# Hybrid attention slots: the product of the probabilities moves ahead of the slot's first delta step

## What is computed

```python
o_a = banded_attention(q_a, k_a, v_a, A_WINDOW, attn_sinks)       # 4 heads, window 128, sink logits
o_b = nsa_mixer(q_b, ...)                                         # 4 heads: compressed, selected, window branch
o_c = gated_delta_net(cqkv, ca, cb, cz, ...)                      # 4 heads of 128, chunks of 64
x = x + gt_m * (concatenate([o_a, o_b, o_c], axis=-1) @ w_out)

# both attentions, for each head and block of 128 queries:
p = softmax(where(mask, q @ k.T * scale, NEG_INF));  o = p @ v

# gated delta rule, for each chunk c of 64 tokens, in sequence:
v_new = u[c] - w[c] @ state
o_c   = q_dec[c] @ state + qk[c] @ v_new
state = state * g_last[c] + k_dec[c].T @ v_new
# before that, u and w come from a triangular solve for each chunk
```

## Time and profile before

| | |
|---|---|
| median of 3 runs | 2823.74 us (2822.07 to 2827.61) |
| the profiled execution's own time | 2822.6 us, its span 2821.1 us |
| PE busy | 2694.4 us (96% of the span) |
| DVE busy | 1626.9 us (58%) |
| ACT busy | 1123.0 us (40%) |
| slots of the first hybrid layer | 1503.2 to 1654.7 us |
| slots of the second hybrid layer | 2243.9 to 2395.4 us |

### The profile page before, as it was taken

The page is one execution under the profiler, slowest core; times in us unless marked ns, Lnnn a source line. Parts: engine busy times, 40 slices in busy tenths (PEclk is TensorE's granted clock), DMA queues, the critical chain, the costliest instruction groups (busy, mean ns, idle before and its releaser), DMA issues.

```text
span 2821.1 us, 41800 instructions
## 1 busy us (share of the span) xinstructions
PE 2694.4 (96%) x17262; PEld 2120.9 (75%) x17262; DVE 1626.9 (58%) x2917; ACT 1123.0 (40%) x1964; POOL 9.4 (0%) x21
## 2 busy tenths in 40 slices
PE   5999999999998999999998899999999988999998
PEld 4776888867666788886886667888878766788886
DVE  6588746573555775667556665444465577533334
ACT  3544324234555442323345553221334466422222
POOL 0000000000000000000000000000000000000000
PEclk9999999999999999999999999999999999999999
DMA  6445555533221365653230013444433200222222
GB/s 255 141 137 173 189 187 173 191 114 108 72 71 58 101 205 195 193 195 129 97 117 28 3 53 127 131 153 141 138 127 102 101 3 3 90 97 97 97 98 82
DMA packets 92093, 336.42 MB, mean 119 GB/s; under 512 B 10480, under 2 KB 10736, under 8 KB 91776
## 3 DMA queue, kind: packets, MB, share of 16 engines
q1 hardware_dynamic: 86800, 315.40, 34.0%
q10 hardware_dynamic: 3792, 14.11, 1.4%
q0 software_dynamic: 1312, 4.23, 0.5%
HBM read 331.57 MB, written 2.13 MB: 118 GB/s over the span
## 4 chain that ended last, share of the span: by engine, by line
PE 46%; ACT 4%; DVE 3%; issue 1%; DVEq 0%; ACTq 0%
PE bank L649 12%; PE bank L651 12%; PE bank L650 12%; ACT probs L2279 1%; PE bank L923 1%; PE bank L908 1%; PE bank L1004 1%; PE bank L894 1%; PE bank L689 0%; PE bank L691 0%; PE bank L690 0%; PE bank L1178 0%; PE bank L977 0%; PE bank L992 0%; PE bank L1188 0%
## 5 line engine op out<-in xcount | busy, mean ns | idle before, releaser
L649 PE MATMUL bank<-in_high,weights_high 128*128 128x512 f32 x1856 | 734.2, 396 | 7.5 <-DVE in_low L1432 3.4
L1283 DVE TENSOR_TENSOR weights_low<-weight_ring,weights_high 128x1024 fp32r<-128x1024 f32 x404 | 493.6, 1223 | 426.5 <-ACT weights_high L2034 426.4
L651 PE MATMUL bank<-in_high,weights_low 128*128 128x512 f32 x1856 | 723.8, 390 | 0.0
L650 PE MATMUL bank<-in_low,weights_high 128*128 128x512 f32 x1856 | 723.6, 390 | 0.0
L2034 ACT ACTIVATE weights_high<-weight_ring 128x1024 fp32r<-128x1024 f32 x404 | 424.3, 1051 | 444.6 <-PE bank L651 299.9
L649 PEld LDWEIGHTS bank<-in_high,weights_high 128*128 128x128 f32 x1856 | 349.1, 188 | 94.8 <-issue 9.3
L650 PEld LDWEIGHTS bank<-in_low,weights_high 128*128 128x128 f32 x1856 | 349.3, 188 | 74.2 <-issue 3.4
L651 PEld LDWEIGHTS bank<-in_high,weights_low 128*128 128x128 f32 x1856 | 348.9, 188 | 73.4
L649 PE MATMUL bank<-hidden_split,weights_high 128*128 128x512 f32 x864 | 336.9, 390 | 0.0
L651 PE MATMUL bank<-hidden_split,weights_low 128*128 128x512 f32 x864 | 336.1, 389 | 0.0
L650 PE MATMUL bank<-hidden_split,weights_high 128*128 128x512 f32 x864 | 336.1, 389 | 0.0
(11 more groups left out here) (390 smaller groups left out, 3309.2 us busy)
## 6 DMA issues: line engine op xcount, KB each, us to landing
weight_ring<-stream SPq DMA_DIRECT2D x597, 512.0 KB, 3.4
mixer_out<-cmp ACTq DMA_DIRECT2D x6, 1024.0 KB, 4.9
hidden<-forget_rows POOLq DMA_DIRECT2D x16, 256.0 KB, 3.5
residual<-x ACTq DMA_DIRECT2D x4, 512.0 KB, 12.5
mixer_out<-cmp SPq DMA_DIRECT2D x2, 1024.0 KB, 6.1
out<-mixer_out ACTq DMA_DIRECT2D x4, 512.0 KB, 2.8
constants<-consts ACTq DMA_DIRECT2D x1, 1821.5 KB, 20.5
silu_c<-c ACTq DMA_DIRECT2D x2, 512.0 KB, 4.3
```

The source lines that it names most:

```text
L649: pe.matmul(bank[:, :], WHI[:, z, cols], high, start=(k == 0), stop=False)
L650: pe.matmul(bank[:, :], WHI[:, z, cols], low, start=False, stop=False)
L651: ins = pe.matmul(bank[:, :], WLO[:, z, cols], high, start=False, stop=(k == ktiles - 1))
L1283: v.tensor_tensor(WLO[:, z, :], ring[:, n % RING, :], WHI[:, z, :].bitcast(F32), ALU.subtract).then_inc(*mark("weights_low", "low", n))
```

## The change

In hybrid slots PE's product no longer stands behind the delta step of part 0 but ahead of it, directly behind the scores. Nothing is added or taken out, and DVE's and ACT's programs are the same. In `fox` the order stays.

```diff
@@ -896,7 +896,8 @@
                         it, w = items[2 * d + z], items[2 * d + z]["width"]
                         pe.matmul(B[2 + z][64:P, 0:w], it["q"][:, 64:P], it["k"], start=True, stop=True).then_inc(
                             *mark("tensor_attention", *name, "scores", 2 * d + z))
-                fill(d, 0)
+                if name[0] != "hyb":
+                    fill(d, 0)
                 if 2 <= d <= n + 1:
                     out_free(d - 2)
                     pair = [(items[i], PT[0:min(P, items[i]["width"]), i % 2, :]) for i in (2 * d - 4, 2 * d - 3)]
...
                     ins.then_inc(*mark("tensor_attention", *name, "product", d - 2))
+                if name[0] == "hyb":
+                    fill(d, 0)
                 fill(d, "behind the product")
                 for z in range(2):
                     if z:
```

## The result

The changed kernel took 2884.39 us, median of four runs (2874.34 to 2885.66), beside 2823.42 of the kernel before on the same chip: ratio 1.0209, with an interval of 1.0196 to 1.0221. It is slower by 61 us. The forecast was 2864 us and its range ended at 2880, so the direction was right and the size was not.

A forecast was written before the change was run, and what follows sets the result against it. A chain between PE, DVE and ACT was taken to bound the hybrid stretches. 18 us a layer for slots 2 to 31 plus 2 for the last made 40, giving 2864 us with the run offset; range 2840 to 2880.

The forecast's parts named there:

- What bounds the stretches: In both hybrid layers' 151.5 us stretches, no engine is full; a chain between PE, DVE and ACT sets the time.
- 0.6 us a slot: In slots 2 to 31, the later delta step costs 0.6 us each on average, 18 us a layer.
- The single walks: Timelines of slots 5, 26 and 28 followed: about 0.7, 1.05 and 0.25 us later, mean 0.67.
- The release: In the walked slots, PE's product starts 0.06 us after the DVE copy ends.
- Slots 32 and 33, 2.0 us a layer: Slot 32 costs nothing; in slot 33 the sum for head 3 starts 2.04 us later, passed on in full.
- The idle time ahead of the product, "about 10" a layer: PE's idle time ahead of the product grows from 1.8 to about 10 us a layer, nearly all ended by the DVE copy.
- The clock: In both stretches, PE's time at the lower level doubles, costing at most 4.5 us a layer: 2873 us, chance 0.05.
- PE's queue alone counts: In the hybrid slots, DVE's and ACT's delays vanish in their holes, leaving 0.3 us a slot: 2843 us, chance 0.10.
- No cover: Upper bound: each hybrid slot's step costs its full delay, mean 1.0 us: 2887 us; no chance of its own given.

The follow-up runs named there:

- the version for the solve slots: Against the kernel before, the product moved ahead of the delta step in slots 2 to 23 alone; 2862.07 us, ratio 1.0142.
- the wait alone: Against the kernel before, only the waits for both copies moved ahead of the delta step, the product staying behind it; 2843.3 us, ratio 1.0076.
- the last slots changed: Against the kernel before, the product moved ahead of the norm's sums in slots 32 and 33 alone; 2827.83 us, ratio 1.0013.
- the parts: The change against the kernel before in slots 2 to 23, 24 to 31, or 32 and 33 alone; 2862.07, 2829.23 and 2827.83 us.

## Why the prediction was right and wrong

- **What bounds the stretches: right.** A chain to and fro between three engines, with the product's time beside it so far. DVE and ACT stayed at the same busy time. That PE would too was wrong, by the clock: with the clock held up or nearly so, and a few matmuls more, PE was busy for 132.6 us a stretch in the old order and for 135.8 and 136.3 in the new one; in the changed kernel, where the clock fell, it was 141 and 143.
- **0.6 us a slot: right as a mean.** In slots 6 to 15 and 17 to 30, 24 in all, where both orders can be compared at full clock (for some of them by the second layer of the version for the solve slots), the new order costs 14.8 us, 0.62 a slot. Slots 2 and 3 cost nothing. With the mean for slots 4, 5, 16 and 31, which can't be compared so, the slots cost 28 x 0.62 = 17.3 us a layer, for 18 predicted. The single walks were less good, and that three of them gave the right mean is in part luck. Slot 26 is longer by 0.35 from scores to scores, for 1.05 predicted; from one DVE copy to the next it is 4.75 for 3.93 (2361.96 in the earlier trace rows to 2365.89), 0.82 more, of which the next scores, which don't wait for the state, take only a part. Slot 28 costs 0.18 (0.25 predicted), slots 29 and 30 0.46 and 1.3. Of the 0.6 the wait alone makes about a half: 10 us a stretch in its own experiment, over 1 of them clock.
- **The release.** I took the product to start 0.06 us behind the copy. It starts 0.15 behind it in slots 5 and 26.
- **Slots 32 and 33, 2.0 us a layer: near.** 3.7 were measured for both, with an interval of 1 to 6. The traces, at nearly the same clock, say more: from the scores of slot 31 in the second layer to the end of the kernel it is 441.7 us with the last slots changed, for 438.9 before, so 2.8 a layer. Counted from those scores the sum for head 3 starts 2.65 us later, for 2.04 predicted, and 0.5 of that is there already when the last product starts: slot 32, which was counted at nothing, costs something too.
- **The idle time ahead of the product, "about 10" a layer: mis-sized.** It is 21.9. The prediction counted the new wait only, but a part of the waits that had stood ahead of the steps, for DVE's and ACT's results, now lies ahead of the product too, as in slot 4. Ahead of L1165, L1178, L1228 and L1110 there were 9.2 us; 3.8 are left ahead of the same lines, and none ahead of L1228, which was foretold. That explains about 5 of the 20 us more. Why the new wait itself is about 15 and not 8 was not looked into.
- **The clock: this is the term that failed.** The prediction took it as 0 in the sum, and as a rival of 4.5 us a layer if the time at the lower level doubled, with 0.05 for it. The row that it read, 0.97 in the earlier trace rows, was right, and so was what it read in slot 5. But that time did not double. It went from 10 to 33 and 40 us within the stretches, 53 us more for both. In the two profiled executions the stretches are 56 us longer. Of these 2 x (17.3 + 1.1) = 37 are delay, 1.1 being the part of the last slots' cost that lies within a stretch. So 19 us are left for the 53: 0.37 each. The two slots, the two layers and the two sets of runs above gave 0.31 to 0.46, and one comparison 0.15. Each microsecond at the lower level thus costs less than the half that PE loses, since in a part of it PE waits anyway. The delay as a whole, 2 x (17.3 + 2.8) = 40 us by the traces, is what the sum had; what it lacked is the clock. The 2 or so that are left of the 61 are the 2.6 us ahead of the first hybrid layer, which the change doesn't touch.

The Trainium skill ("TensorE: Matmul & The Clock Gate", section on the second failure mode, queue depth cycling through PSUM) warns of such a swing. The prediction cited it and gave it too little. The trace agrees: at full clock the product takes 0.66 us as before, and the stretches have six and five falls for two. In its section on how such a swing bites in real kernels the same page of the Trainium skill counts the loss, for a kernel that waits for transfers, as half of the time at the lower level. That would be 26 us for the 53 here; the measurement, 19, decides.

The rivals: that PE's queue alone counts is out, since slots are longer by twice the 0.3 that it would give, and DVE's waits (12.7 us ahead of L1955) carry it. "No cover", at 2887, was nearest in number and wrong in its reason: at full clock a slot costs 0.62, not 1.0, and with the clock nearly level the change costs 35 to 38 us, not 64. That the two errors of "no cover", too much delay and no clock, come to about the measured time is luck.

**What stays open** is what decides whether the clock falls in a given slot. In the version for the solve slots, slots 7 to 9 are equally long in both layers to 0.01 us, and behind them the clock fell in one layer and not in the other. The layers were not alike before that, though: slots 4 and 5 had two falls of 3.4 us in the first and one of 10.2 in the second. Nor does PE's idle time alone decide it: 28 us of it in a stretch went with 13.7 us at the lower level where only the wait was ahead, 30 and 31 with 7 and 3 where a matmul stood in each solve slot, and 39 and 37 with 33 and 40 in the changed kernel. That the parts add up to 50 and the whole to 61 fits the changing number of falls: the version for the solve slots had 34.1 and 20.5 us at the lower level in its stretches, the whole change 33.2 and 40.0. The number of falls was measured in each version, not derived.

## What to carry to other kernels

In a queue written out by hand, a wait placed ahead of independent work costs twice: the wait itself, and the lateness of everything that reads the work behind it. Walk a few slots along both queues and take the mean; single slots can be off by three times, the mean was within 5% here. Then look at the granted clock in the window: where PE has holes and the clock is already a little under 1, a change that lengthens the holes may multiply the time at the lower level, so give it a term in the sum and a wide upper end, with a price from two instances of one slot at either level.

## What was not expected of the hardware

- Idle times ahead of the products, in each stretch one of 3.45 us and all others between 0.1 and 1.6, together 23 and 22 us in stretches of 179 and 180, went with 33 and 40 us at the lower of the two levels (1.2 GHz for 2.4), where 1.8 us ahead of the products had gone with 10.2.
- Eight runs of one program differ by 14 us (2872.46 to 2886.7), with their mean clock (0.987 to 0.981).
- Matmuls that compute nothing can make the kernel faster: 16 of them brought the changed one from 2882.6 to 2871.0 us. In the order of before, matmuls that took the falls away brought nothing (2823.59 for 2823.74).
- A product waits 0.15 us from the end of a DVE copy to its start (slots 5 and 26).
